# Modulation products: four output tiles side by side in TensorE's column groups, one turn per four tiles

## The chip, the cores and the metric

The kernel runs on one core of a Trainium2 chip. The metric is the device time of one execution in microseconds (us), lower being better; the median of several runs is compared. The engines named below are TensorE (PE, its weight loads shown apart as PEld), VectorE (DVE), ScalarE (ACT), GpSimd (POOL) and the queue of SyncE (SPq) that issues the loads.

## The reference, cut to what matters

The reference is a first block (a mixer and a product-key layer of 128 x 128 experts) for 256 tokens, and after it a second block of two layers whose norms and residuals are modulated by two conditioning vectors. Only the modulation matters here:

```python
silu_c = jax.nn.silu(c)            # [1, 1024]
silu_cc = jax.nn.silu(c_ctx)       # [1024]
for i in range(DEPTH_2):           # two layers
    mod_l = (silu_c @ ada_w[i] + ada_b[i])[:, None, :]       # ada_w[i] is 1024 x 6144
    mod_c = (silu_cc @ ada_w[i] + ada_b[i])[None, None, :]
    sh1_l, sc1_l, g1_l, sh2_l, sc2_l, g2_l = jnp.split(mod_l, N_MOD, axis=-1)
    ...
```

So two rows of 1024 numbers are multiplied by a matrix of 1024 x 12288 float32 (48 MB), and the result has to stand in the kernel as columns: `mod[p, layer, block, s]`, 128 outputs across the partitions, `s` being the conditioning vector.

## The kernel before, in words

All weights come through one ring of four buffers, `raw[:, g % 4, :]`, each piece 128 partitions x 1024 float32 (512 KB), in one fixed order that `add_pieces` writes out (L236 to L284). The queue of SyncE issues a piece as soon as the piece four places before it has been used (L287 to L298). Most pieces are "split": ACT rounds them into `whi` (L310), DVE subtracts into `wlo` (L316), and the high and low parts are multiplied by high and low parts of the activations, three matmuls for each product (L494 to L496, L1690 to L1692).

The expert layer is two long stages of 128 groups each. In the key stage (L1427 to L1661) a group is one piece of `peer_u_t`: 24 matmuls of 128 x 256 into one of three banks, then a gelu by ACT (L1511, L1513) which frees the bank; DVE picks the best keys and experts in between (L1560 to L1634), and from group 62 on PE also routes one-hot products (L1482). In the value stage (L1669 to L1733) a group is one piece of `peer_v_t`, 24 matmuls that add into banks 0 to 3; ACT and DVE make `gh` and `gl` from the gated values (L1713, L1726).

The modulation products are woven into these two stages, since their weights come from the same ring. `ada_w` is cut in 24 output tiles of 512 columns. A tile has eight chunks of 128 inputs, in four pieces; a piece holds two chunks x 512 outputs. `KEY_ADA` and `VALUE_ADA` (L75, L76) say behind which group half a tile is worked: 16 halves in the key stage (tiles 0 to 7, every 3.4 groups from group 3), 32 in the value stage (tiles 8 to 23, every 3.6 groups from group 2).

A half (`half_pe`, L698 to L710) is two raw pieces and four matmuls in plain float32. The stationary operand is one chunk of the conditioning vectors, padded from 2 to 32 columns; the moving operand is 512 weights wide. The four matmuls go to the four column groups, that is to PSUM partitions 0, 32, 64 and 96 of one bank, by chunk: chunk `c` goes to group `c % 4`. So after both halves each column group holds a quarter of the sum. ACT copies the bank to SBUF (`row_act`, L726). Then `turn_pe` (L690 to L696) multiplies each 128 columns of this copy by a 0/1 matrix with two columns, which adds the four quarters and turns rows to columns: four matmuls with 128 x 128 stationary and 2 columns moving. The turn of tile `t - 1` follows the second half of tile `t`; the last turn of each stage stands alone two groups after the last half. `out_act` (L728 to L732) copies the columns to `mod` once in each stage.

What waits on what: PE waits for its two raw pieces (L705), for `ada_rows_out` before it writes a bank that it used two tiles ago and before it turns; ACT waits for PE's `raw_used` before its row copy. In the trace every float32 matmul shows as two records, so a half is 8 records of L709, and a turn 8 records of L695.

Of the kernel before, what the change touches and what calls it, by code (L numbers as in the profile page):

```python
# [60 lines left out]
ROPE_THETA = 10000.0  # L61
TT = T + TC

ADA_TILES = LAYERS * N_MOD * D // 512
ADA = (8, ADA_TILES)
KEY_LOT, VALUE_LOT = range(len(ADA))
COLS = 32

# [3 lines left out]
SPLIT = 3  # L72


KEY_ADA = {3 + n * 34 // 10: [(n // 2, n % 2)] for n in range(2 * ADA[KEY_LOT])}  # L75
VALUE_ADA = {2 + n * 36 // 10: [(ADA[KEY_LOT] + n // 2, n % 2)] for n in range(2 * (ADA[VALUE_LOT] - ADA[KEY_LOT]))}  # L76
BATCH = 4
SLICE = 1650
EXP_AT, TURN_AT = 54, 61
# [14 lines left out]
    NV += _w  # L94


CONSTS = [("ident", P), ("ones", P), ("ones64", P), ("iota", P), ("group", 32), ("rows", NSA_G)]
MIX_CONSTS = [("hg_mask", P), ("dist", TB * T), ("cbias", NSA_HEADS * TB * N_CMP), ("cmask", TB * NSA_G * N_CMP)]
CONST_AT, NCONST = {}, 0
for _n, _w in CONSTS:  # L100
# [8 lines left out]
def const_tables():  # L109

    t = {}
    i = np.arange(P)
    t["ident"] = np.eye(P)
    t["ones"] = np.ones((P, P))
    t["ones64"] = (i[:, None] // 64 == i[None, :] // 64) * 1.0
    t["iota"] = np.broadcast_to(i, (P, P))

    t["group"] = (i[:, None] % 32 == np.arange(32)[None, :]) * 1.0
    t["rows"] = (i[:, None] // 32 == np.arange(NSA_G)[None, :]) * 1.0

    s = np.zeros((P, P))
    for m in range(P):
        k = m + 16 if m % 32 < 16 else m - 16
        s[k, m] = -1.0 if m % 32 < 16 else 1.0
    t["swap"] = s

    t["hg_mask"] = ((i[:, None] <= i[None, :]) & (i[:, None] // HG_CHUNK == i[None, :] // HG_CHUNK)) * 1.0
    pos = np.arange(T)
    dist = (pos[:, None] - pos[None, :]).astype(np.float64)

    t["dist"] = np.where(dist >= 0, -dist, NEG).reshape(TB, P, T).transpose(1, 0, 2).reshape(P, -1)
    end = np.arange(N_CMP) * CMP_STRIDE + CMP_LEN - 1
    cd = (pos[:, None] - end[None, :]).astype(np.float64)
    near = np.where(cd >= 0, -cd, NEG).astype(np.float32).reshape(TB, P, 1, N_CMP)
    slopes = (2.0 ** (-8.0 * (np.arange(NSA_HEADS) + 1) / NSA_HEADS)).astype(np.float32).reshape(2, NSA_G, 1)
    t["cbias"] = (near.transpose(1, 0, 2, 3)[:, None] * slopes[None, :, None]).reshape(P, -1)
    t["cmask"] = np.broadcast_to((cd >= 0).reshape(TB, P, 1, N_CMP) * 1.0, (TB, P, NSA_G, N_CMP)).transpose(1, 0, 2, 3).reshape(P, -1)
    half = DH // 2
    inv = (1.0 / (np.float32(ROPE_THETA) ** (np.arange(0, half, 2, dtype=np.float32) / np.float32(half)))).astype(np.float32)
    row = (pos // GRID_W).astype(np.float32)  # L140
    col = (pos % GRID_W).astype(np.float32)
    ang = np.concatenate([np.tile((row[:, None] * inv).T, (2, 1)), np.tile((col[:, None] * inv).T, (2, 1))])
    t["cos"] = np.tile(np.cos(ang), (2, 1))
    t["sin"] = np.tile(np.sin(ang), (2, 1))
    t["rope"] = np.concatenate([t["cos"], t["sin"], t["swap"]], axis=1)

    def table(names):
        return np.ascontiguousarray(np.concatenate([t[n] for n in names], axis=1).astype(np.float32))
    return table([n for n, _ in CONSTS]), table([n for n, _ in MIX_CONSTS]), table(["rope"])

# [14 lines left out]
def build(nc, dr):  # L165

    ctx = ExitStack()
    with ctx:
        def sem(name):
            return ctx.enter_context(nc.semaphore(name))  # L170
# [73 lines left out]
            return first  # L244


        ada_at = [[] for _ in range(ADA_TILES)]

        def add_half(t, half):
            first = add_pieces("ada_t", False, 4 * t + 2 * half, 4 * t + 2 * half + 2)  # L250
            ada_at[t].extend((first, first + 1))

        top_pe = sem("top_pe_step")
        at_in, at_cmp = [], []
        for w in dr["w_in_t"]:
# [7 lines left out]
        at_keys = add_pieces("peer_keys_t", split=False, end=lambda i: (top_pe, 4 * i + 4))  # L263
        for i in range(2, PK_KEYS):
            at_u.append(add_pieces("peer_u_t", a=i, b=i + 1))
            for h in KEY_ADA.get(i - 2, ()):
                add_half(*h)
        at_v = []
        for i in range(PK_KEYS):
            at_v.append(add_pieces("peer_v_t", a=i, b=i + 1))  # L270
            for h in VALUE_ADA.get(i - 2, ()):
                add_half(*h)
        at_ple = add_pieces("ple_gate_t")
        add_pieces("ple_proj_t")
        at_qkv = [None] * LAYERS
# [25 lines left out]
        def piece_loaded(eng, g):  # L301
            eng.wait_ge(raw_loaded[g % RAW], 16 * (g // RAW + 1))
# [378 lines left out]
        class AdaLot:  # L681
# [3 lines left out]
            def __init__(self, lot, cond, rows, banks):  # L685
                self.a, self.b = ADA[lot - 1] if lot else 0, ADA[lot]
                self.cond, self.rows, self.banks = cond, rows, banks
                self.end = ada_at[self.b - 1][-1] + 1

            def turn_pe(self, pe, t):  # L690

                pe.wait_ge(ada_rows_out, t + 1)
                for j in range(4):
                    n = 4 * (t - self.a) + j
                    mm = pe.matmul(ps[:, self.banks[2], 2 * n:2 * n + 2], self.rows[:, t % 2, j * P:j * P + P], k("group", 0, 2), start=True, stop=True)  # L695
                mm.then_inc(ada_turned, 1)  # L696

            def half_pe(self, pe, t, half):  # L698


                if half == 0 and t >= self.a + 2:
                    pe.wait_ge(ada_rows_out, t - 1)
                for i in (2 * half, 2 * half + 1):
                    g = ada_at[t][i]
                    piece_loaded(pe, g)  # L705
                    for j in range(2):
                        c = 2 * i + j
                        q = COLS * (c % 4)
                        mm = pe.matmul(ps[q:q + COLS, self.banks[t % 2], :], self.cond[:, c, :], raw[:, g % RAW, j * 512:j * 512 + 512],  # L709
                                       start=(c < 4), stop=(c >= 4), tile_position=(0, q))  # L710
                    mm.then_inc(raw_used, 1)

            def pe(self, pe):
                for t in range(self.a, self.b):
                    for half in range(2):
                        self.half_pe(pe, t, half)
                    if t > self.a:
                        self.turn_pe(pe, t - 1)
                self.turn_pe(pe, self.b - 1)

            def row_act(self, act, t):

                act.wait_ge(raw_used, pieces[ada_at[t][3]][3] + 1)
                if t >= self.a + 2:
                    act.wait_ge(ada_turned, t - 1)
                act.activation(self.rows[:, t % 2, :], ps[:, self.banks[t % 2], :], ACT.Copy).then_inc(ada_rows_out, 1)  # L726

            def out_act(self, act):  # L728
                a, b = self.a, self.b
                act.wait_ge(ada_turned, b)  # L730
                act.activation(mod[:, :, :, :].rearrange("p l j s -> p (l j s)")[:, 8 * a:8 * b], ps[:, self.banks[2], 0:8 * (b - a)],
                               ACT.Copy).then_inc(ada_out.h, 1)  # L732

            def act(self, act):
                for t in range(self.a, self.b):
                    self.row_act(act, t)
                self.out_act(act)


        mixer = ctx.enter_context(ExitStack())  # L740
# [686 lines left out]
        with nc.Block() as block:  # L1427
# [5 lines left out]
            def _(pe):  # L1433
# [9 lines left out]
                for i in range(GROUPS):  # L1443
# [12 lines left out]
                    if i == min(KEY_ADA):  # L1456
                        pe.wait_ge(top_act, 8)
                        pe.wait_ge(cond_padded, 2)
                    for t, half in KEY_ADA.get(i, ()):
                        key_lot.half_pe(pe, t, half)  # L1460
                        if half and t > key_lot.a:
                            key_lot.turn_pe(pe, t - 1)
                    if i == max(KEY_ADA) + 2:
                        key_lot.turn_pe(pe, key_lot.b - 1)
# [22 lines left out]
            def _(act):  # L1487
# [11 lines left out]
                        ins = act.activation(ohs[:, r % 2, 1, q, :], ohs[:, r % 2, 1, q, :], ACT.Copy, scale=wT[:, t:t + 1])  # L1499
                    ins.then_inc(hot_weighted, 1)  # L1500
                for i in range(GROUPS):
                    for t, half in KEY_ADA.get(i - 1, ()):
                        if half:
                            key_lot.row_act(act, t)
                    if i == max(KEY_ADA) + 3:
                        key_lot.out_act(act)
                    act.wait_ge(piece_used, nu + i + 1)
# [161 lines left out]
        with ExitStack() as own, nc.Block() as block:  # L1669
# [11 lines left out]
            def _(pe):  # L1681
                for i in range(GROUPS):
# [10 lines left out]
                    mm.then_inc(piece_used, 1)  # L1693
                    if i == min(VALUE_ADA):
                        pe.wait_ge(late_cond, 2)
                    for t, half in VALUE_ADA.get(i, ()):
                        value_lot.half_pe(pe, t, half)
                        if half and t > value_lot.a:
                            value_lot.turn_pe(pe, t - 1)
                    if i == max(VALUE_ADA) + 2:  # L1700
                        value_lot.turn_pe(pe, value_lot.b - 1)
# [1 line left out]
            @block.scalar  # L1703
            def _(act):
                for i in range(GROUPS):
                    for t, half in VALUE_ADA.get(i - 3, ()):
                        if half:
                            value_lot.row_act(act, t)
                    if i == max(VALUE_ADA) + 5:
                        value_lot.out_act(act)  # L1710
                    if i >= 3:
# [526 lines left out]
def _layouts(a):  # L2238
# [30 lines left out]
    o["peer_v_t"] = np.ascontiguousarray(f["peer_v"][0].reshape(PK_KEYS, PK_KEYS, D).transpose(1, 0, 2))  # L2269
    o["ple_gate_t"] = _tiles(f["ple_gate_w"][0])  # L2270
    o["ple_proj_t"] = _tiles(f["ple_proj"][0])
    o["ada_t"] = np.concatenate([_tiles(f["ada_w_2"][i]) for i in range(LAYERS)])
    o["qkv0_t"] = _tiles(f["na_w_qkv_2"][0])
    o["o0_t"] = _tiles(f["na_w_o_2"][0])
    g = f["gqa_w_qkv_2"][0]
# [50 lines left out]
```

## Time and profile before

| | |
|---|---|
| median of 3 runs | 2252.4 us (2251.59 to 2254.49) |
| the profiled execution, own time | 2255.02 us |
| its span | 2253.2 us |
| its mean granted TensorE clock | 0.973 |
| PE busy | 2130.6 us (95%) |
| DVE busy | 1252.7 us (56%) |
| ACT busy | 1033.1 us (46%) |
| load traffic | 325.76 MB read, 145 GB/s over the span |

Busy times are of one profiled execution. A matmul record is longer than the time by which it holds up the next one, since matmuls are pipelined (most records of 128 x 256 last 0.28 us and follow each other every 0.12 us), so the cost of a matmul is read from starts, not from durations. PE's "busy 95%" says where it has no gap, and the stages have to be looked at one by one.

### The profile page before, as it was taken

To read this page: it belongs to the slowest core of one execution; us is meant where nothing else is said; L and a number is where in the kernel's file an instruction comes from. 1 tells how busy PE (TensorE), PEld (TensorE's weight loads), DVE (VectorE), ACT (ScalarE), POOL (GpSimd) and SP (SyncE) were. 2 spreads that over 40 slices of the span, in tenths; PEclk is the share of its full clock that TensorE was granted. 3 is DMA by queue.
4 is the path that set the end of the run, shared out by engine and by line. 5 is a ranking of instruction groups with operands and counts; after the bars stand their busy time and mean duration, and the time that the engine had idled before them with its cause. 6 is when DMAs were issued, how large, how long until landed. Compare 5 with 4: busy or idle time off the path is not lost. (4 is left out here: it accounts for less than half of the span.)

```text
span 2253.2 us, 36524 instructions
## 1 busy us (share of the span) xinstructions
PE 2130.6 (95%) x15218; PEld 1892.8 (84%) x15218; DVE 1252.7 (56%) x1943; ACT 1033.1 (46%) x1914; POOL 7.0 (0%) x10
## 2 busy tenths in 40 slices
PE   7888999999999999999988999989999998899998
PEld 6768999999998999999986876768887887479997
DVE  6675588877887445445455237553333225556544
ACT  5664444467775444444444227442322215455443
POOL 0000000000000000000000000000000000100000
PEclk9988999999999999999989999999999999899999
DMA  6503577744443777777644210123222223014543
GB/s 206 189 1 129 175 256 246 252 168 141 141 141 122 247 246 246 249 250 238 233 162 154 95 66 1 57 75 103 92 97 92 94 85 118 1 58 150 187 172 109
DMA packets 91252, 329.18 MB, mean 146 GB/s; under 512 B 10064, under 2 KB 12496, under 8 KB 90832
## 3 DMA queue, kind: packets, MB, share of 16 engines
q1 hardware_dynamic: 91088, 326.84, 42.6%
q8 instruction: 121, 1.98, 0.4%
q14 instruction: 43, 0.35, 0.1%
HBM read 325.76 MB, written 1.05 MB: 145 GB/s over the span
## 5 line engine op out<-in xcount | busy, mean ns | idle before, releaser
L316 DVE TENSOR_TENSOR wlo<-raw,whi 128x1024 fp32r<-128x1024 f32 (+1 forms) x502 | 612.2, 1221 | 604.0 <-ACT whi L310 599.9
L310 ACT ACTIVATE whi<-raw 128x1024 fp32r<-128x1024 f32 (+1 forms) x502 | 527.1, 1052 | 485.0 <-PE ps L496 460.4
L494 PE MATMUL ps<-x_hi,whi 128*128 128x512 f32 (+1 forms) x1040 | 360.4, 347 | 28.1 <-DVE x_lo L477 22.6
L495 PE MATMUL ps<-x_lo,whi 128*128 128x512 f32 (+1 forms) x1040 | 359.3, 345 | 0.0
L496 PE MATMUL ps<-x_hi,wlo 128*128 128x512 f32 (+1 forms) x1040 | 358.8, 345 | 0.0
L494 PE MATMUL ps<-xT_hi,whi 128*128 128x256 f32 x1152 | 334.0, 290 | 4.1 <-DVE xT_lo L475 4.1
L495 PE MATMUL ps<-xT_lo,whi 128*128 128x256 f32 x1152 | 326.7, 284 | 0.0
L496 PE MATMUL ps<-xT_hi,wlo 128*128 128x256 f32 x1152 | 326.7, 284 | 0.0
L1690 PE MATMUL ps<-gh,whi 128*128 128x256 f32 x1024 | 294.1, 287 | 5.6 <-DVE gl L1726 5.6
L1691 PE MATMUL ps<-gl,whi 128*128 128x256 f32 x1024 | 290.8, 284 | 0.0
L1692 PE MATMUL ps<-gh,wlo 128*128 128x256 f32 x1024 | 290.7, 284 | 0.0
L494 PEld LDWEIGHTS ps<-x_hi,whi 128*128 128x128 f32 x1040 | 202.1, 194 | 53.8 <-issue 31.5
L494 PEld LDWEIGHTS ps<-xT_hi,whi 128*128 128x128 f32 x1152 | 221.7, 192 | 12.1 <-issue 11.2
L495 PEld LDWEIGHTS ps<-xT_lo,whi 128*128 128x128 f32 x1152 | 221.9, 193 | 0.0
L496 PEld LDWEIGHTS ps<-xT_hi,wlo 128*128 128x128 f32 x1152 | 221.6, 192 | 0.0
L496 PEld LDWEIGHTS ps<-x_hi,wlo 128*128 128x128 f32 x1040 | 202.0, 194 | 22.7
L495 PEld LDWEIGHTS ps<-x_lo,whi 128*128 128x128 f32 x1040 | 202.1, 194 | 21.9
L1690 PEld LDWEIGHTS ps<-gh,whi 128*128 128x128 f32 x1024 | 197.6, 193 | 20.0 <-issue 20.0
L1691 PEld LDWEIGHTS ps<-gl,whi 128*128 128x128 f32 x1024 | 197.7, 193 | 0.0
L1692 PEld LDWEIGHTS ps<-gh,wlo 128*128 128x128 f32 x1024 | 197.6, 193 | 0.0
L1713 ACT ACTIVATE gh<-gated 128x256 fp32r<-128x256 f32 x128 | 53.0, 416 | 192.6 <-PE ps L1692 190.4
L1726 DVE TENSOR_TENSOR gl<-gated,gh 128x256 fp32r<-128x256 f32 x128 | 54.4, 426 | 140.5 <-ACT gh L1713 140.5
(346 smaller groups left out, 3088.1 us busy)
## 6 DMA issues: line engine op xcount, KB each, us to landing
raw<-peer_u_t SPq DMA_DIRECT2D x128, 512.0 KB, 3.3
raw<-peer_v_t SPq DMA_DIRECT2D x128, 512.0 KB, 4.3
raw<-ada_t SPq DMA_DIRECT2D x96, 512.0 KB, 5.3
raw<-ffn_in_t SPq DMA_DIRECT2D x88, 512.0 KB, 3.2
raw<-ffn_out_t SPq DMA_DIRECT2D x44, 512.0 KB, 3.2
raw<-qkv_t SPq DMA_DIRECT2D x36, 512.0 KB, 3.3
raw<-w_in_t SPq DMA_DIRECT2D x24, 512.0 KB, 3.7
raw<-peer_wq_t SPq DMA_DIRECT2D x16, 512.0 KB, 3.3
```

The costliest lines, as they stand in the source:

```text
L310: act.activation(whi[:, n % SPLIT, 0:w], raw[:, g % RAW, 0:w], ACT.Copy).then_inc(hi_done, 1)
L316: dve.tensor_tensor(wlo[:, n % SPLIT, 0:w], raw[:, g % RAW, 0:w], whi[:, n % SPLIT, 0:w].bitcast(F32), ALU.subtract).then_inc(lo_done, 1)
L494: pe.matmul(place, wh, xh, start=start, stop=False, skip_group_check=shared)
L495: pe.matmul(place, wh, xl, start=False, stop=False, skip_group_check=shared)
L496: return pe.matmul(place, wl, xh, start=False, stop=stop, skip_group_check=shared)
L1690: pe.matmul(place, w[0], gh[:, i % 3, :], start=(i == 0 and c % 2 == 0), stop=False, skip_group_check=True)
L1691: pe.matmul(place, w[0], gl[:, i % 3, :], start=False, stop=False, skip_group_check=True)
L1692: mm = pe.matmul(place, w[1], gh[:, i % 3, :], start=False, stop=(i == GROUPS - 1), skip_group_check=True)
L1713: act.activation(gh[:, i % 3, :], gbuf[:, i, :], ACT.Copy).then_inc(gates_hi, 1)
L1726: dve.tensor_tensor(gl[:, i % 3, :], gbuf[:, i, :], gh[:, i % 3, :].bitcast(F32), ALU.subtract).then_inc(gates_lo, 1)
```

## The change

The same products are laid out another way. Four output tiles (2048 outputs, a "quad") are worked together, six quads in all, two in the key stage and four in the value stage. A piece now holds one chunk of 128 inputs x 1024 outputs, that is two tiles' worth. A unit is two such pieces and four matmuls with the same stationary chunk, one for each tile of the quad, each in its own column group. Over the eight units of a quad every column group adds up its own whole sum. The row copy and the turn come once in a quad; the turn's 0/1 matrix has eight columns ("spots", which picks rows 32q and 32q + 1), so it gives 128 outputs x 4 tiles x 2 vectors in one matmul. The places of the units (`KEY_ADA`, `VALUE_ADA`), the number and size of the pieces, and their order in the ring are those of the halves. The copy to `mod` is one ACT instruction per quad, with a strided view. The table of constants grows by 8 columns. On the host the weights are laid out for it.

```diff
-ADA_TILES = LAYERS * N_MOD * D // 512
-ADA = (8, ADA_TILES)
+QUAD = 4 * 512
+QUADS = LAYERS * N_MOD * D // QUAD
+ADA = (2, QUADS)
...
-KEY_ADA = {3 + n * 34 // 10: [(n // 2, n % 2)] for n in range(2 * ADA[KEY_LOT])}
-VALUE_ADA = {2 + n * 36 // 10: [(ADA[KEY_LOT] + n // 2, n % 2)] for n in range(2 * (ADA[VALUE_LOT] - ADA[KEY_LOT]))}
+KEY_ADA = {3 + n * 34 // 10: divmod(n, C) for n in range(C * ADA[KEY_LOT])}
+VALUE_ADA = {2 + n * 36 // 10: divmod(C * ADA[KEY_LOT] + n, C) for n in range(C * (ADA[VALUE_LOT] - ADA[KEY_LOT]))}
...
+    t["spots"] = (i[:, None] == 32 * (n // 2) + n % 2) * 1.0
...
+            def unit_pe(self, pe, t, c):
+                if c == 0 and t >= self.a + 2:
+                    pe.wait_ge(ada_rows_out, t - 1)
+                for i in range(2):
+                    g = ada_at[t, c] + i
+                    piece_loaded(pe, g)
+                    for j in range(2):
+                        q = COLS * (2 * i + j)
+                        mm = pe.matmul(ps[q:q + COLS, self.banks[t % 2], :], self.cond[:, c, :], raw[:, g % RAW, j * 512:j * 512 + 512],
+                                       start=(c == 0), stop=(c == C - 1), tile_position=(0, q))
+                    mm.then_inc(raw_used, 1)
...
             def turn_pe(self, pe, t):
                 pe.wait_ge(ada_rows_out, t + 1)
                 for j in range(4):
-                    n = 4 * (t - self.a) + j
-                    mm = pe.matmul(ps[:, self.banks[2], 2 * n:2 * n + 2], self.rows[:, t % 2, j * P:j * P + P], k("group", 0, 2), start=True, stop=True)
+                    at = 32 * (t - self.a) + 8 * j
+                    mm = pe.matmul(ps[:, self.banks[2], at:at + 8], self.rows[:, t % 2, j * P:j * P + P], k("spots"), start=True, stop=True)
                 mm.then_inc(ada_turned, 1)
...
-                act.activation(mod[:, :, :, :].rearrange("p l j s -> p (l j s)")[:, 8 * a:8 * b], ps[:, self.banks[2], 0:8 * (b - a)],
-                               ACT.Copy).then_inc(ada_out.h, 1)
+                for t in range(a, b):
+                    to = mod[:, :, :, :].rearrange("p l j s -> p (l j s)")[:, 32 * t:32 * t + 32].rearrange("p (q j s) -> p q j s", q=4, j=4)
+                    got = ps[:, self.banks[2], 32 * (t - a):32 * (t - a) + 32].rearrange("p (j q s) -> p q j s", j=4, q=4)
+                    ins = act.activation(to, got, ACT.Copy)
+                ins.then_inc(ada_out.h, 1)
...
-                    for t, half in KEY_ADA.get(i, ()):
-                        key_lot.half_pe(pe, t, half)
-                        if half and t > key_lot.a:
+                    if i in KEY_ADA:
+                        t, c = KEY_ADA[i]
+                        key_lot.unit_pe(pe, t, c)
+                        if c == 1 and t > key_lot.a:
                             key_lot.turn_pe(pe, t - 1)
...
-                    for t, half in KEY_ADA.get(i - 1, ()):
-                        if half:
-                            key_lot.row_act(act, t)
+                    if i - 1 in KEY_ADA and KEY_ADA[i - 1][1] == C - 1:
+                        key_lot.row_act(act, KEY_ADA[i - 1][0])
```

The value stage is changed in the same way, its row copy standing three groups behind the unit as before. `row_act` waits for the last piece of chunk 7.

## Rows read from the trace of the kernel before

**Rows 1.** The page's slices: 40 equal parts of the span, busy tenths, granted clock.

```profile
PE   7888999999999999999988999989999998899998
PEclk9988999999999999999989999999999999899999
```

**Rows 2.** Stages: busy us (x instructions) of each engine, clock, DMA share, GB/s.

```profile
260.00:457.00 197.00, 197.00 (x1623) 181.46 (x1623) 163.05 (x464) 90.80 (x135) 0.00 (x0) 1.00 0.73 247
457.00:724.00 267.00, 261.55 (x2220) 261.34 (x2218) 211.58 (x272) 184.57 (x532) 0.00 (x0) 1.00 0.41 141
735.00:1113.00 378.00, 378.00 (x3102) 346.91 (x3102) 187.05 (x227) 162.62 (x242) 0.00 (x0) 1.00 0.73 247
1149.00:2253.00 1104.00, 1028.89 (x6154) 858.89 (x6154) 499.88 (x678) 435.75 (x727) 6.84 (x6) 0.96 0.28 97
```

**Rows 3.** All instructions of the turn's line: ns min/median/max, first and last start.

```profile
L695 PE MATMUL ps<-kon,values_rows x128: 169/251/272, 768.9 to 1112.8; 128*128 128x2 f32 x128
L695 PE MATMUL ps<-kon,gated x64: 169/251/272, 311.2 to 456.3; 128*128 128x2 f32 x64
```

**Rows 4.** PE in order of time (start us, us): a half without a turn.

```profile
745.13 0.28 PE L1692 MATMUL ps<-gh,wlo 128*128 128x256 f32 x1
745.34 1.07 PE L709 MATMUL ps<-raw,values_cond 128*32 128x512 f32 x8
746.34 0.38 PE L1690 MATMUL ps<-gh,whi 128*128 128x256 f32 x1
746.56 0.28 PE L1691 MATMUL ps<-gl,whi 128*128 128x256 f32 x1
746.68 0.28 PE L1692 MATMUL ps<-gh,wlo 128*128 128x256 f32 x1
```

**Rows 5.** PE in order of time: a half with a turn behind it.

```profile
767.65 0.28 PE L1692 MATMUL ps<-gh,wlo 128*128 128x256 f32 x1
767.86 1.07 PE L709 MATMUL ps<-raw,values_cond 128*32 128x512 f32 x8
768.86 1.05 PE L695 MATMUL ps<-kon,values_rows 128*128 128x2 f32 x8
769.77 0.36 PE L1690 MATMUL ps<-gh,whi 128*128 128x256 f32 x1
769.98 0.28 PE L1691 MATMUL ps<-gl,whi 128*128 128x256 f32 x1
770.09 0.28 PE L1692 MATMUL ps<-gh,wlo 128*128 128x256 f32 x1
```

**Rows 6.** PE in order of time: a turn that stands alone.

```profile
455.48 0.28 PE L496 MATMUL ps<-xT_hi,wlo 128*128 128x256 f32 x1
455.60 0.95 PE L695 MATMUL ps<-kon,gated 128*128 128x2 f32 x8
456.41 0.36 PE L494 MATMUL ps<-xT_hi,whi 128*128 128x256 f32 x1
...
456.73 0.28 PE L496 MATMUL ps<-xT_hi,wlo 128*128 128x256 f32 x1
```

**Rows 7.** PE in order of time: four float32 matmuls with 128 columns moving.

```profile
478.09 0.28 PE L496 MATMUL ps<-xT_hi,wlo 128*128 128x256 f32 x1
478.21 1.06 PE L1482 MATMUL ps<-one_hots 128*128 128x128 f32 x8
479.02 0.36 PE L494 MATMUL ps<-xT_hi,whi 128*128 128x256 f32 x1
```

**Rows 8.** PE, 50.8 to 52.6 us: float32 matmuls of 512 columns, full width.

```profile
50.91 1.88 PE L820 MATMUL ps<-head_rstd,kon 128*128 128x512 f32 x4
```

**Rows 9.** ACT's row copy and final copy, each line's instructions.

```profile
L726 ACT ACTIVATE values_rows<-ps x16: 597/597/602, 746.5 to 1105.5; 128x512 f32<-128x512 f32 x16
L731 ACT ACTIVATE mod<-ps x2: 216/246/277, 457.0 to 1113.1; 128x64 f32<-128x64 f32 x1, 128x128 f32<-128x128 f32 x1
```

**Rows 10.** Waits, value stage then key stage: us in total, times, longest us.

```profile
ACT gh L1713 <- PE ps L1692: 170.5, 97, 2.7
ACT whi L310 <- DMA raw<-peer_v_t: 2.6, 4, 1.8
...
ACT whi L310 <- DMA raw<-peer_u_t: 7.0, 11, 0.8
```

**Rows 11.** DVE and PE in order of time around value group 12.

```profile
761.44 1.23 DVE L316 TENSOR_TENSOR wlo<-raw,whi 128x1024 fp32r<-128x1024 f32 x1 [2.41 <-ACT whi L310]
764.89 0.28 PE L1690 MATMUL ps<-gh,whi 128*128 128x256 f32 x1
```

**Rows 12.** Two modulation pieces: their issue (with time to landing), and their use.

```profile
999.40 1.62 SPq L298 DMA_DIRECT2D raw<-ada_t  x2
raw<-ada_t SPq DMA_DIRECT2D x2, 512.0 KB, 7.1
1007.55 0.28 PE L1692 MATMUL ps<-gh,wlo 128*128 128x256 f32 x1
1007.76 1.11 PE L709 MATMUL ps<-raw,values_cond 128*32 128x512 f32 x8
```

**Rows 13.** DVE at the end of its selection work, which PE needs at 468.00 us.

```profile
462.80 0.43 DVE L1633 TENSOR_TENSOR gated<-gated 128x256 f32<-128x256 f32 x1
463.80 1.23 DVE L316 TENSOR_TENSOR wlo<-raw,whi 128x1024 fp32r<-128x1024 f32 x1 [0.58 <-ACT whi L310]
```

More of the change, by code:

```diff
@@ L94 @@
     NV += _w
-CONSTS = [("ident", P), ("ones", P), ("ones64", P), ("iota", P), ("group", 32), ("rows", NSA_G)]
+CONSTS = [("ident", P), ("ones", P), ("ones64", P), ("iota", P), ("group", 32), ("rows", NSA_G), ("spots", 8)]
 MIX_CONSTS = [("hg_mask", P), ("dist", TB * T), ("cbias", NSA_HEADS * TB * N_CMP), ("cmask", TB * NSA_G * N_CMP)]
@@ L118, in const_tables @@
     t["group"] = (i[:, None] % 32 == np.arange(32)[None, :]) * 1.0
+    n = np.arange(8)
+    t["spots"] = (i[:, None] == 32 * (n // 2) + n % 2) * 1.0
     t["rows"] = (i[:, None] // 32 == np.arange(NSA_G)[None, :]) * 1.0
@@ L244, in add_pieces, with add_unit @@
             return first
[L247 to L251, printed above, removed]
+        ada_at = {}
+        def add_unit(u):
+            t, c = u
+            ada_at[u] = add_pieces("ada_t", False, 2 * (C * t + c), 2 * (C * t + c) + 2)
         top_pe = sem("top_pe_step")
@@ L265, in build @@
             at_u.append(add_pieces("peer_u_t", a=i, b=i + 1))
-            for h in KEY_ADA.get(i - 2, ()):
-                add_half(*h)
+            if i - 2 in KEY_ADA:
+                add_unit(KEY_ADA[i - 2])
         at_v = []
@@ L270, in build @@
             at_v.append(add_pieces("peer_v_t", a=i, b=i + 1))
-            for h in VALUE_ADA.get(i - 2, ()):
-                add_half(*h)
+            if i - 2 in VALUE_ADA:
+                add_unit(VALUE_ADA[i - 2])
         at_ple = add_pieces("ple_gate_t")
@@ L687, in __init__ @@
                 self.cond, self.rows, self.banks = cond, rows, banks
-                self.end = ada_at[self.b - 1][-1] + 1
+            def unit_pe(self, pe, t, c):
[9 more added lines that the diff above has]
+                    mm.then_inc(raw_used, 1)
             def turn_pe(self, pe, t):
@@ L693, in turn_pe @@
                 for j in range(4):
-                    n = 4 * (t - self.a) + j
-                    mm = pe.matmul(ps[:, self.banks[2], 2 * n:2 * n + 2], self.rows[:, t % 2, j * P:j * P + P], k("group", 0, 2), start=True, stop=True)
+                    at = 32 * (t - self.a) + 8 * j
+                    mm = pe.matmul(ps[:, self.banks[2], at:at + 8], self.rows[:, t % 2, j * P:j * P + P], k("spots"), start=True, stop=True)
                 mm.then_inc(ada_turned, 1)
[L698 to L719, printed above, removed]
             def row_act(self, act, t):
-                act.wait_ge(raw_used, pieces[ada_at[t][3]][3] + 1)
+                act.wait_ge(raw_used, pieces[ada_at[t, C - 1] + 1][3] + 1)
                 if t >= self.a + 2:
@@ L730, in out_act @@
                 act.wait_ge(ada_turned, b)
-                act.activation(mod[:, :, :, :].rearrange("p l j s -> p (l j s)")[:, 8 * a:8 * b], ps[:, self.banks[2], 0:8 * (b - a)],
-                               ACT.Copy).then_inc(ada_out.h, 1)
[L734 to L737, printed above, removed]
+                for t in range(a, b):
[3 more added lines that the diff above has]
+                ins.then_inc(ada_out.h, 1)
         mixer = ctx.enter_context(ExitStack())
@@ L1695, in _ @@
                         pe.wait_ge(late_cond, 2)
-                    for t, half in VALUE_ADA.get(i, ()):
-                        value_lot.half_pe(pe, t, half)
-                        if half and t > value_lot.a:
+                    if i in VALUE_ADA:
+                        t, c = VALUE_ADA[i]
+                        value_lot.unit_pe(pe, t, c)
+                        if c == 1 and t > value_lot.a:
                             value_lot.turn_pe(pe, t - 1)
@@ L1705, in _ @@
                 for i in range(GROUPS):
-                    for t, half in VALUE_ADA.get(i - 3, ()):
-                        if half:
-                            value_lot.row_act(act, t)
+                    if i - 3 in VALUE_ADA and VALUE_ADA[i - 3][1] == C - 1:
+                        value_lot.row_act(act, VALUE_ADA[i - 3][0])
                     if i == max(VALUE_ADA) + 5:
@@ L2271, in _layouts @@
     o["ple_proj_t"] = _tiles(f["ple_proj"][0])
-    o["ada_t"] = np.concatenate([_tiles(f["ada_w_2"][i]) for i in range(LAYERS)])
+    ada = np.concatenate([f["ada_w_2"][i] for i in range(LAYERS)], axis=1)
+    o["ada_t"] = np.ascontiguousarray(ada.reshape(C, P, QUADS, 2, 2 * 512).transpose(2, 0, 3, 1, 4).reshape(-1, P, PIECE))
     o["qkv0_t"] = _tiles(f["na_w_qkv_2"][0])
```

## The prediction, made before the changed kernel ran

> **What bounds the kernel now.** I went from the page's slices to the stages, then to single instructions. The slices show TensorE (PE) nearly full everywhere, and full where the modulation products run [rows 1]. By stage, PE is busy for 197.00 of 197.00 us in the key stage's part with halves and for 378.00 of 378.00 us in the value stage's, at the full granted clock (1.00, the 2.4 GHz level), while DVE has 163.05 and 187.05 us, ACT 90.80 and 162.62 us, and the loads take 0.73 of the DMA engines' time [rows 2]. The reader should see that no other engine is near its limit there and that PE has no gap at all. The order of time confirms it: matmuls of 128 x 256 start every 0.12 us, and what stands between two groups is a half, a turn, or nothing [rows 4 to 6]. So in these two stretches the time is the sum of PE's instructions, and anything taken from PE is gained, as long as nothing else is late by then.
>
> **What the change removes: 18 turns.** The trace has 128 records of the turn's line in the value stage and 64 in the key stage [rows 3]; a turn is 8 records, so there are 16 and 8 turns, 24 in all. After the change there is one for each quad: 4 and 2. Twelve turns go from the value stage and six from the key stage. All 18 are of the kind that stands behind a half; the two at the ends, which stand alone, stay.
>
> **The price of a turn** comes from starts, since durations overlap. A half without a turn: from the last matmul of the group before it (745.13) to the third of the group after it (746.68) are 1.55 us, where three steps of 0.12 would be 0.36, so a half costs 1.19 us [rows 4]. With a turn the same stretch goes from 767.65 to 770.09, 2.44 us, so half and turn cost 2.08 us [rows 5]. The difference, the turn, is 0.89 us. The turn that stands alone gives the same: 455.48 to 456.73 is 1.25 us, less 0.36 is 0.89 us [rows 6]. The agreement matters: the turn costs what it costs whether it follows a half or not, so nothing of it stays behind with the half. The rows shown are typical of all 26 halves without and 22 with a turn. 18 x 0.89 = 16.0 us.
>
> The Trainium skill's page "TensorE: Matmul & The Clock Gate", section "LDWEIGHTS (loading the stationary operand)", puts a weight load at its columns divided by 1.2, in ns. By that, a turn's eight loads of 128 columns would be 8 x 107 = 0.85 us, and the gain, called an estimate, 15.4 us. The trace's 0.89 us decides.
>
> **What it adds to the turns that stay: eight moving columns for two.** The trace has no such matmul. Bounds: a float32 matmul with 2 columns on the one side, one with 128 on the other. Four of the latter (one-hot products) take the stretch from 478.09 to 479.02, 0.93 us [rows 7]; the lone turn has the same 0.93 us from 455.48 to 456.41 [rows 6]. Both ends are equal, so eight columns cost nothing more. Six turns stay; the term is zero.
>
> **What it changes in the 48 halves, now units.** Number, size, places and column groups of the matmuls stay: four in a row to partitions 0, 32, 64, 96 of one bank. New are that all four load the same stationary chunk, and that seven of eight units add to the bank where it was one of two halves. In the value stage every matmul from the second group on adds to its bank, and it keeps the 0.12 us of the key stage's, whose groups begin afresh [rows 4, 6]. So adding is free at that shape. For loading one chunk four times the trace has no row; the nearest is a half itself, four chunks in four groups, 1.19 us. A gain is excluded, since the same 512 columns have to stream; the upper bound is the loss of the overlap among column groups. Full-width float32 matmuls of 512 columns follow each other with four records in 1.88 us, of which the last runs out in 0.59: (1.88 - 0.59) / 3 = 0.43 us each [rows 8]. Eight records in a row would be 3.4 us, 2.2 us more for each unit. I take zero, since the row that is nearest is the same instruction at the same places.
>
> **What it takes from ACT.** 18 of 24 row copies of 0.60 us, some 10.7 us, and it makes six final copies of 32 columns where there were two, of 64 and 128 columns in 0.22 and 0.28 us [rows 9]; so at most 6 x 0.28 = 1.7 us. None of it shows. ACT sat idle 170.5 us for PE in the value stage [rows 10], and the copies' cover is that wait. The four final copies of the value stage, at most 1.1 us where 0.28 was, stand ahead of `gh` and a `whi` in ACT's queue, and DVE and PE wait for those; they meet a PE that is ahead of nothing, because the split weights are ready 2.2 us or more before their group. Without that cover they would cost about 0.8 us once.
>
> **The waits.** No wait is new. PE still waits for a row copy before a turn, two units after the last product of that tile, some seven groups, and ACT needs 0.60 us for it. PE's wait on a bank used two tiles ago becomes one on a bank used two quads ago, which is longer past. Nothing is moved past SPq or POOL; the ring has the same 96 pieces in the same order.
>
> **What is late next.** With 16 us less on PE, the followers have less time. First the split weights: at value group 12 `wlo` is done at 761.44 + 1.23 = 762.67 and PE comes at 764.89, a margin of 2.2 us, the smallest of that stage; the usual one is 3 to 5 us [rows 11]. ACT had waited 1.8 us for a transfer there, the longest of four such waits [rows 10]. Second, the modulation pieces themselves, which have no buffer ahead. At the tightest place the second was issued at 999.40 + 1.62 - 0.33 = 1000.7, took 7.1 us and so landed at 1007.8, just as PE came for it: 1007.76 where a half normally follows 0.21 us after the last matmul, and the records took 1.11 for 1.07 us [rows 12, 4]. That place, and every second half, has no turn since the half before it, and so shows what all will be like after the change. PE lost 0.05 us there and nothing at the other 23. So removing turns makes the other half of the places like those that already hold without loss. Mean traffic goes from 247 GB/s to 247 x 575 / 559 = 254 GB/s [rows 2]. Third, DVE's selection work, which PE needs for its transposes at 468.00: it is done at 462.80 + 0.43 = 463.23, 4.8 us earlier, and DVE follows PE there, waiting for `whi` after it [rows 13]. PE will be 6 x 0.89 = 5.3 us earlier at that point, but DVE's pace is set by PE's through each `whi`, and it waited for ACT again and again on the way; its 163.05 us of work fit into 197.0 - 5.3 = 191.7 us [rows 2].
>
> **The sum.** The profiled execution took 2255.02 us and would take 2239.0. It is 2.6 us above the median of 2252.4, so the median would be 2252.4 - 16.0 = 2236.4 us.
>
> **What shakes it.** After the value stage the clock is 0.96 over 1104 us [rows 2], that is 88 us at the 1.2 GHz level in several stretches, each behind a wait of PE. All of this comes 16 us earlier, and a stretch may end sooner or later. The three runs differ by 2.9 us without any change. I allow 2.5 us to either side. The Trainium skill ("TensorE: Matmul & The Clock Gate", "What you observe") says likewise that the moment of the rise differs from run to run; no row here tells its share.
>
> **Rivals.**
> (a) *The transfers take part of it back.* For it: one piece landed as PE came [rows 12], and landings vary. Against: 23 of 24 like places had time to spare. If a quarter of the 48 units waited 0.5 us, 6 us would be lost: 2242 us. Chance 0.10.
> (b) *The loads set the pace after all*, and the two stretches cannot shrink: 2252 us. Against: 0.73 of the DMA engines' time, and ACT's waits for transfers are only 2.6 and 7.0 us, with no gap on PE behind them [rows 2, 10]. This is also the case that the change does nothing. Chance 0.02.
> (c) *Slower: the four column groups no longer overlap in a unit*, because all four load the same chunk. Price 2.2 us for each of 48 units, 106 us: 2342 us; it decides from (16.0 + 4.5) / 48 = 0.43 us for each unit. Against: column groups, bank and order are those of before, where the overlap is seen: eight records of 0.6 us in 1.07 us [rows 4]. Chance 0.03.
> (d) *More than forecast*: the half-clock stretches get shorter, and PE's margins elsewhere with them: 2231 us. Chance 0.05.
> The forecast itself: 0.80, with a range of 2234 to 2239.
>
> **How the numbers follow.** The likeliest is 2236.4. Taking in the run-to-run spread, a part of (a) and a part of (d), the range is 2232 to 2241. A measurement of this kernel can tell about 0.2% from no change, 4.5 us. Faster: 0.80 + 0.10 + 0.05 = 0.95, of which I give 0.01 to same for a stronger form of (a); same 0.03, slower 0.03 make the rest.
>
> **What the profile after would show.** L695's successor has 48 records in place of 192, with unchanged 0.93 us stretches; halves still cost 1.19 us; both stretches stay at 100% PE, the value part about 10.7 us and the key part 5.3 us shorter; traffic near 254 GB/s; everything behind the value stage unchanged but for the clock. Gaps on PE ahead of the unit's matmuls would speak for (a), a longer unit for (c). The prediction is wrong if either appears in more than a few units.

## The result, and the profile after

The changed kernel takes 2222.8 us (median of 4 runs, 2219.66 to 2224.46) against 2253.4 us before (4 runs on the same occasion, 2251.59 to 2255.33). The ratio is 0.9861, with a 95% interval of 0.9845 to 0.9876. It is 30.7 us faster, nearly twice the 16.0 us that were forecast, and below the forecast range, whose lower end was 2232.

| | before | after |
|---|---|---|
| profiled execution, own time, us | 2255.02 | 2222.13 |
| its span, us | 2253.2 | 2220.4 |
| PE busy, us | 2130.6 | 2098.9 |
| ACT busy, us | 1033.1 | 1030.9 |
| instructions | 36524 | 36186 |
| mean granted clock | 0.973 | 0.974 |

The page after, its slices as in [rows 1], and three stretches as in [rows 2]:

```profile
PE   7888999999998999999979999989999998899998
PEclk9998999999999999999989999999999999899999
```

```profile
260.00:457.00 197.00, 197.00 (x1644) 180.54 (x1643) 170.07 (x466) 91.75 (x135) 0.00 (x0) 1.00 0.75 251
735.00:1113.00 378.00, 374.22 (x3126) 344.05 (x3126) 199.48 (x244) 169.99 (x248) 0.00 (x0) 1.00 0.76 252
1149.00:2253.00 1104.00, 1003.20 (x5927) 817.99 (x5925) 477.02 (x640) 417.85 (x693) 6.85 (x6) 0.97 0.28 92
```

The stretches have the bounds of before, so that they now hold more of the work. What to see is the first: PE is full for 197.00 us as it was, but holds 1644 matmul records instead of 1623, although turns are gone. (A turn is 8 records in 0.89 us, denser than a group, so fewer turns alone would lower the count.) The second is not full because the value stage is over at 1107.9 us. The third ends beyond the kernel's end.

The turn, as in [rows 3], and one that stands alone, as in [rows 6]:

```profile
L711 PE MATMUL ps<-kon,values_rows x32: 173/256/277, 816.6 to 1074.2; 128*128 128x8 f32 x32
L711 PE MATMUL ps<-kon,gated x16: 172/256/277, 368.6 to 442.4; 128*128 128x8 f32 x16
```

```profile
441.55 0.28 PE L499 MATMUL ps<-xT_hi,wlo 128*128 128x256 f32 x1
441.67 0.95 PE L711 MATMUL ps<-kon,gated 128*128 128x8 f32 x8
442.48 0.36 PE L497 MATMUL ps<-xT_hi,whi 128*128 128x256 f32 x1
```

There are 48 records for 192, six turns for 24, and from 441.55 to 442.48 the stretch still takes 0.93 us with eight columns. A unit, as in [rows 4]:

```profile
771.42 0.28 PE L1683 MATMUL ps<-gh,wlo 128*128 128x256 f32 x1
771.63 1.06 PE L702 MATMUL ps<-raw,values_cond 128*32 128x512 f32 x8
772.62 0.39 PE L1681 MATMUL ps<-gh,whi 128*128 128x256 f32 x1
772.85 0.28 PE L1682 MATMUL ps<-gl,whi 128*128 128x256 f32 x1
772.97 0.28 PE L1683 MATMUL ps<-gh,wlo 128*128 128x256 f32 x1
```

From 771.42 to 772.97 are 1.55 us, as with a half before. So the parts that the prediction costed are as it said. What is new is in the groups themselves, which the change does not touch. First and last matmul of key group 26, before and then after:

```profile
351.23 0.28 PE L494 MATMUL ps<-xT_hi,whi 128*128 128x256 f32 x1
...
353.99 0.28 PE L496 MATMUL ps<-xT_hi,wlo 128*128 128x256 f32 x1
```

```profile
342.75 0.28 PE L497 MATMUL ps<-xT_hi,whi 128*128 128x256 f32 x1
...
345.44 0.28 PE L499 MATMUL ps<-xT_hi,wlo 128*128 128x256 f32 x1
```

The 23 steps from the first to the 24th matmul take 2.76 us before and 2.69 after, 0.120 and 0.117 us each. The duration of one matmul, 0.28 us, does not show it; only the starts do. Taken over all some 2900 undisturbed steps of each stage, the mean goes from 119.8 to 116.8 ns in the key stage and from 119.9 to 116.8 in the value stage.

Where the 32.8 us of the two profiled spans are, by the starts of first and last matmuls: before the projection of the keys 4.7 us, in that projection 1.1, in the key stage 13.3 (452.05 to 438.74), in the value stage 20.4 (423.26 to 402.85); and the second block takes 6.6 us more (1095.77 to 1102.35). So part of the gain lies ahead of the modulation products, where nothing was changed, and the second block, where nothing was changed either, lost.

The clock has a share in it that the mean granted clock, 0.973 and 0.974, hardly shows. The profile's clock records put 123.7 us of the span before at the 1.2 GHz level and 115.8 us of the span after. These 7.9 us less are worth at most half as much, 4.0 us, where PE was busy, since that level is half the other; 2.5 of them fall into the value stage and 3.7 into the second block. Of the 4.7 us ahead of the projection, the shorter step explains some 1.6: 615 undisturbed steps of 256 columns there take 119.8 ns before and 117.2 after. The rest is not shown to be the change's, since that part of the kernel varies from run to run: where its buffers lie as before, it took 209.4 us here, and 210.4, 207.0, 208.9 and 207.7 in the profiled executions of `no_shift`, `shift256`, `shift512` and `moving32` below.

### The profile page after: what moved, and what is told of

Read it like the earlier page. It is cut to its first block and busy times, and to the rows that moved or that the text cites. A ratio compares the mean times of both kernels' runs of the same rounds, so it can differ in the third digit from the quotient of the medians.

```text
span 2220.4 us, 36186 instructions
## 1 busy us (share of the span) xinstructions
PE 2098.9 (95%) x15074; PEld 1844.0 (83%) x15074; DVE 1250.9 (56%) x1943; ACT 1030.9 (46%) x1900; POOL 7.1 (0%) x10
## 5 line engine op out<-in xcount | busy, mean ns | idle before, releaser
L497 PE MATMUL ps<-ffn_hi,whi 128*128 128x512 f32 (+1 forms) x352 | 119.8, 340 | 6.2 <-PEq L541 6.2
```

Source lines behind the costliest of these rows:

```text
L497: pe.matmul(place, wh, xh, start=start, stop=False, skip_group_check=shared)
```

## The experiments

The change does one thing besides what its text is about: the table of constants, `kon`, gets 8 columns, so every buffer placed behind it starts 32 bytes later. The ring `raw` and the split weights `whi` and `wlo` lie ahead of it and stay. Theory A was that these 32 bytes make the matmuls quicker; theory B that the new products or the missing turns do.

**The shift without the change.**

```diff
-CONSTS = [..., ("group", 32), ("rows", NSA_G)]
+CONSTS = [..., ("group", 32), ("rows", NSA_G), ("unused", 8)]
```

> The kernel before with 8 unused columns in the table of constants: all buffers allocated behind it start 32 bytes later, as in the changed kernel; the halves and the 24 turns are those of before. Theory A (the 32 bytes make the 128x256 matmuls follow each other faster): their step falls from 0.120 to 0.117 us in the key and value stages, some 6100 matmuls x 0.003 = 18 us there, and the time is about 2253.4 - 14.4 = 2239 us, with the turns still at 0.89 us each. Theory B (the faster step comes from the new products or from having fewer turns): step 0.120 us and 2253 us.

Measured: 2238.4 us (4 runs), ratio 0.9940 (0.9917 to 0.9962). The key stage took 442.95 us, the value stage 414.47, the mean steps were 116.8 and 116.9 ns. Value group 97, first and last matmul:

```profile
1027.85 0.28 PE L1691 MATMUL ps<-gh,whi 128*128 128x256 f32 x1
...
1030.53 0.28 PE L1693 MATMUL ps<-gh,wlo 128*128 128x256 f32 x1
```

It takes 2.68 us for 23 steps, with all 24 turns in place. That is what theory A expected.

**The change without the shift.** The eight columns of the 0/1 matrix are columns of the identity, which is in the table already.

```diff
-CONSTS = [..., ("rows", NSA_G), ("spots", 8)]
+CONSTS = [..., ("rows", NSA_G)]
...
-  mm = pe.matmul(ps[:, self.banks[2], at:at + 8], self.rows[...], k("spots"), start=True, stop=True)
+  mm = pe.matmul(ps[:, self.banks[2], at:at + 8].rearrange("p (q s) -> p q s", s=2), self.rows[...],
+                 k("ident").rearrange("p (q r) -> p q r", r=COLS)[:, :, 0:2], start=True, stop=True)
```

> The changed kernel, its 0/1 matrix taken as a strided view of the identity that is in the table anyway (columns 32q and 32q + 1), so that no column is added and every buffer starts where it does in the kernel before. Theory A: the step of the 128x256 matmuls is back at 0.120 us, only the 18 turns are gone, 2253.4 - 16.0 = 2237.4 us. Theory B: 0.117 us and 2223 us, as the changed kernel.

Measured: 2237.1 us (4 runs) beside 2254.7 before, ratio 0.9926 (0.9906 to 0.9947). The same group:

```profile
1037.09 0.28 PE L1680 MATMUL ps<-gh,whi 128*128 128x256 f32 x1
...
1039.85 0.28 PE L1682 MATMUL ps<-gh,wlo 128*128 128x256 f32 x1
```

2.76 us for 23 steps, mean 119.8 and 119.9 ns. So the change proper gives what the prediction said it would, and the shift gives the rest. The two ratios multiply to 0.9940 x 0.9926 = 0.9866, the changed kernel's 0.9861.

**Which distance counts.** Four larger shifts, one kernel that moves weights and activations alike, and one that moves the weights alone:

> The kernel before with 16 unused columns in the table, a shift of 64 bytes. If what matters is the start within 64 bytes, the step is back at 0.120 us and the time at 2253 us. If any other start than that of before is faster, the step is 0.117 us and the time about 2239 us.

> The kernel before with 32 unused columns, a shift of 128 bytes for everything behind the table. If the distance counts modulo 256, as the looks at 256 and 512 bytes suggest, the key stage takes 446 us or less and the step is below 0.118 us; if it counts modulo 128, 0.120 us and 452 us.

> The kernel before with 64 unused columns, a shift of 256 bytes for everything behind the table. The distance between weights and activations was a multiple of 512 bytes. If only a multiple of 512 is slow, the step is 0.117 or 0.118 us and the key stage about 445 us; if multiples of 256 are, 0.120 us and 452 us.

> The kernel before with 128 unused columns, a shift of 512 bytes. The chunks of the weights are 512 bytes apart and those of the activations 1024, and the step was 0.120 us for all of them; so if the distance modulo 512 matters, the step is 0.120 us again and the key stage 452 us. If every shift helps, 0.117 us and 443 to 446 us.

```diff
# all32
+        ctx.enter_context(nc.sbuf_tensor("unused", [P, 8], F32))
         raw = ctx.enter_context(nc.sbuf_tensor("raw", [P, RAW, PIECE], F32))
```

> The kernel before with 32 unused bytes ahead of the ring of weights: the weights (stationary) and the activations (moving) both start 32 bytes later, so their distance is that of before. If the distance between the two operands matters, the step stays at 0.120 us and the time at 2253 us. If the moving operand's own start matters, the step is 0.117 us and the time about 2239 us.

```diff
# weights32
+        idle = ctx.enter_context(nc.sbuf_tensor("idle", [P, 1], F32))
         whi = ctx.enter_context(nc.sbuf_tensor("whi", [P, SPLIT, PIECE], F32R))
...
-        idle = ctx.enter_context(nc.sbuf_tensor("idle", [P, 1], F32))
```

> The kernel before, with one small buffer (idle) moved from behind the table to ahead of the split weights whi and wlo: the weights, the stationary operand, start 32 bytes later, and the activations start where they did. If the distance between the two operands matters, the step of the 128x256 matmuls falls to about 0.117 us and the key stage from 452 to about 443 us. If the moving operand's own start matters, 0.120 us and 452 us.

The table gives the mean step in the key stage (256 columns moving, some 2900 steps), the mean step of the matmuls with 512 columns moving over split weights in the second block (some 2160 steps), and the stages' times in us, all from the starts in each trace. The last column is one run where no median is named:

| activations against weights | 256 cols, ns | 512 cols, ns | key stage | second block | us |
|---|---|---|---|---|---|
| as before | 119.8 | 226.8 | 452.05 | 1095.8 | 2253.4 (median) |
| both +32 bytes (all32) | 119.8 | 226.8 | 452.04 | 1094.1 | 2249.9 |
| +32 (shift32) | 116.8 | 233.3 | 442.95 | 1099.9 | 2238.4 (median) |
| +64 (shift64) | 117.6 | 228.9 | 445.60 | 1089.8 | 2234.4 |
| +128 (shift128) | 119.3 | 232.6 | 450.28 | 1105.1 | 2256.7 |
| +256 (shift256) | 119.8 | 226.7 | 452.04 | 1095.8 | 2252.6 |
| +512 (shift512) | 119.8 | 226.8 | 452.04 | 1095.9 | 2255.0 |
| -32 (weights32) | 118.3 | 233.3 | 447.16 | 1105.1 | 2249.3 |

The steps can be compared as they stand. The times of the second block can't, since its time at the 1.2 GHz level differs too: 75.2 us before, but 64.3 with the shift of 32 bytes, 65.4 with 64 and 69.2 in `all32`, against 70.9 to 75.2 in the other four. So some 5 of the 6.0 us that the second block gains at 64 bytes go with the clock, and the 2234.4 us, one run, are not a price of the distance alone. Why the clock fell less often there is open.

Value group 97 with a shift of 256 bytes, and with everything moved by 32:

```profile
1046.36 0.28 PE L1691 MATMUL ps<-gh,whi 128*128 128x256 f32 x1
...
1049.12 0.28 PE L1693 MATMUL ps<-gh,wlo 128*128 128x256 f32 x1
```

```profile
1045.29 0.28 PE L1691 MATMUL ps<-gh,whi 128*128 128x256 f32 x1
...
1048.05 0.28 PE L1693 MATMUL ps<-gh,wlo 128*128 128x256 f32 x1
```

It is 2.76 us both times. The step does not hang on the activations' own address, since 32 bytes for all change nothing, and 32 bytes for the weights alone do. It hangs on the distance between weights and activations, and it has the old values again at 256 and 512 bytes, so the distance counts modulo 256 as far as these shifts tell; modulo 128 is excluded by the 232.6 ns at 128 bytes. Before, it was an exact multiple: by the buffers' addresses in the program `xT_hi` started 159744 bytes behind `whi`, 624 x 256, and `gh` lay at the same place as `xT_hi`. At 128 bytes I expected a step below 0.118 us if 256 was the period, and that was a miss: 119.3 ns.

What is good for 256 columns is bad for 512. Two matmuls of the second block 24 steps apart, before and then with the shift of 32 bytes:

```profile
1503.83 0.39 PE L494 MATMUL ps<-x_hi,whi 128*128 128x512 f32 x1
...
1509.27 0.39 PE L494 MATMUL ps<-x_hi,whi 128*128 128x512 f32 x1
```

```profile
1483.08 0.39 PE L495 MATMUL ps<-x_hi,whi 128*128 128x512 f32 x1
...
1488.68 0.39 PE L495 MATMUL ps<-x_hi,whi 128*128 128x512 f32 x1
```

These are 5.44 and 5.60 us, 226.7 and 233.3 ns a step. The second block has some 2350 undisturbed steps of 512 columns and 2200 of 256, so the shift costs it 2350 x 6.5 = 15.3 us and gives 2200 x 3.1 = 6.8. The difference is 8.5 us. The changed kernel's second block took 6.6 us more, beside 3.7 us less at the 1.2 GHz level, which hid up to 1.8 us of it: 8.4 us together.

**The moving operand alone.** To tell the operands of the matmul from the other buffers behind the table, above all the gated values that ACT and DVE write meanwhile:

```diff
+        pb("unused1", [P, 8])
         ffn_norm.parts = xH = [pb(n, [P, C, T], F32R) for n in ("xT_hi", "xT_lo")]
...
+            own.enter_context(nc.sbuf_tensor("unused2", [P, 8], F32))
             gh = own.enter_context(nc.sbuf_tensor("gh", [P, 3, T], F32R))
```

> The kernel before with 32 unused bytes ahead of the two moving operands alone, xT_hi and xT_lo in the key stage, gh and gl in the value stage. Every other buffer of the two stages starts where it did, the gated values and the second block's among them. If it is the distance between moving operand and weights, the step is 0.117 us in both stages, the key stage takes 443 us and the value stage 414 us, and the whole 2253 - 9.1 - 8.8 - 1.0 for the projection ahead of them = 2234 us, the second block staying at 1096 us. If it is the place of another buffer (the gated values, which ACT and DVE write), 0.120 us and 2253 us.

Measured: 2232.8 us (4 runs), ratio 0.9909 (0.9892 to 0.9925). Key stage 443.26 us, value stage 415.57, steps 116.8 and 117.0 ns; the second block's steps are 120.0 and 226.8 ns, unchanged. The gated values, the ring and the split weights had not moved. By the program's addresses some small buffers had, other than the expectation says: those placed behind the two operands (`keyT`, `wT` and `one_hots` in the key stage, `values_rows` and `values_cond` in the value stage). The last two are read only in halves and turns, while the step is shorter in the groups between them. `moving32`, `weights32` and `all32` together leave the distance between the moving operand and the weights.

**Only the low parts.**

```diff
-        ffn_norm.parts = xH = [pb(n, [P, C, T], F32R) for n in ("xT_hi", "xT_lo")]
+        ffn_norm.parts = xH = [pb("xT_hi", [P, C, T], F32R)]
+        pb("unused1", [P, 8])
+        xH.append(pb("xT_lo", [P, C, T], F32R))
...
+            own.enter_context(nc.sbuf_tensor("unused2", [P, 8], F32))
             gl = own.enter_context(nc.sbuf_tensor("gl", [P, 3, T], F32R))
```

> The kernel before with only the low parts, xT_lo and gl, 32 bytes later; the high parts stay. Of the three matmuls of a product (whi with the high part, whi with the low part, wlo with the high part) only the second streams a shifted operand. If a matmul that streams holds up the load of the next one's weights by their distance, the step behind or onto this one matmul is shorter than 0.120 us and the others stay; a third of the gain, some 3 us for each stage (449 and 420 us). If the pace is set by something common to all, all three steps change or none.

Measured: 2235.2 us, key stage 446.24, value stage 415.49. The three steps of a product in the key stage, in order: 117.9, 119.6 and 116.2 ns, where all were 119.6 to 120.1 before. In the value stage they are 117.1, 118.3 and 116.1 ns, for 119.8 to 120.0 before. So moving the operand of one matmul in three changed two of the steps in one stage and all three in the other, and the gain is two thirds in the key stage and nearly all in the value stage. Neither expectation fits; which read holds up which stays open.

**Can both be had?** Two kernels. The first is the changed one at 64 bytes, where 256 columns gain and 512 lose little:

```diff
-CONSTS = [..., ("rows", NSA_G), ("spots", 8)]
+CONSTS = [..., ("rows", NSA_G), ("spots", 8), ("unused", 8)]
```

> The changed kernel with 8 unused columns more in the table, so that the buffers behind it start 64 bytes later than in the kernel before and 32 later than in the changed one. If the two effects add up: the single look at a shift of 64 bytes gave 2234.4 us with the old products, less 16.0 us for 18 turns is 2218 us, some 4 us below the changed kernel's 2222.8. If the turns and the shift share a gain (a rival: the faster step leaves other work late, so that part of a turn's time is lost), nearer to 2223 us or above.

Measured: 2219.0 us (4 runs), ratio 0.9855 (0.9831 to 0.9878). The second has no column added, and 32 bytes at the head of the two scopes that end before the second block:

```diff
         mixer = ctx.enter_context(ExitStack())
+        mixer.enter_context(nc.sbuf_tensor("unused1", [P, 8], F32))
...
         peer = ctx.enter_context(ExitStack())
+        peer.enter_context(nc.sbuf_tensor("unused2", [P, 8], F32))
```

> The changed products with the view of the identity (no column added), and 32 unused bytes at the head of the first block's buffers and of the expert layer's, which are given back before the second block's are placed. So the first block and the expert layer have their activations 32 bytes off the weights' multiple of 256, and the second block has them on it. If the shift is a gain for 256 columns moving and a loss for 512, as the looks at 32 bytes show (0.120 to 0.117 us, but 0.226 to 0.233 us), the second block keeps its 1096 us and the rest is that of the changed kernel: 2222.8 - 6.6 = 2216 us. If the 6.6 us had another cause (the clock's stretches), 2223 us.

Measured: 2219.1 us (5 runs, 2213.41 to 2220.70), ratio 0.9844 (0.9827 to 0.9860). Its steps are 116.7 and 116.8 ns in the key and value stages and 226.7 ns for 512 columns, and the second block takes 1095.5 us. So the 6.6 us came back where they were expected. The whole is 3 us above the expectation, of which 2.4 are in the part ahead of the projection (207.1 us against 204.7 in the changed kernel). The traces say where: the same matmul starts at 114.5 and 114.2 us, and a later one at 141.3 and 138.6, and from 114 to 142 us the mean granted clock is 0.82 here and 0.93 there. So these 2.4 us go with the clock and not with the placing. The intervals of these two and of the changed kernel overlap; none of the three is shown to be the fastest.

## Why the prediction was wrong, point by point

**The bound.** Right. PE's records leave no gap in the two stages, but for late pieces that only the starts show (below), and what was taken from it was gained.

**18 turns at 0.89 us.** Right. 48 records are left. The kernel with the turns gone and nothing shifted took 2237.1 us where 2236.4 was forecast, and on its own occasion 17.6 us less than before, with an interval of 12 to 21 from the ratio. The lone turn costs what it did [rows 6].

**Eight moving columns for nothing.** Right: the stretch of the lone turn is 0.93 us, as with 2 and with 128 columns [rows 6, 7].

**The unit at a half's price.** Right: 1.55 us from 771.42 to 772.97, as in [rows 4]. Rival (c), the loss of the overlap, did not come.

**ACT.** Right as far as it shows: its row copies fell from 24 to 6, and no wait for a row copy appeared on PE.

**What is late next.** Rival (a) came in a small size. In the changed kernel PE stood before or within three units for their second piece, 1.92 us in all; without the shift, in six units, 2.84 us; with all 24 turns in place and the shift of 32 bytes in one, 0.16 us, and in the kernel before in one, 0.05 us. The trace names the transfer:

```profile
L702 PE MATMUL ps<-raw,gated x128: 592/605/617, 271.8 to 435.4; 128*32 128x512 f32 x128
its engine sat idle before it (us, times) until:
  DMA raw<-ada_t: 1.5, 3
```

The longest of them, PE in order of time; the second piece was issued at 307.27 and took 6.7 us:

```profile
312.89 0.28 PE L499 MATMUL ps<-xT_hi,wlo 128*128 128x256 f32 x1
313.10 1.95 PE L702 MATMUL ps<-raw,gated 128*32 128x512 f32 x8
```

It is 1.95 us for 1.07. The argument that the places without a turn ahead of them already show what all will be like [rows 12] was too kind: two intervals without a turn in a row leave less time to catch up than one did. That is a reading, and the late pieces alone don't show it: kernels with all 24 turns lost between nothing and 1.42 us (`moving32`, three units) in one trace each, those with six turns between 1.11 (`after64`) and 2.84 us. ACT's waits for transfers in 735 to 1113 us say it more clearly, where [rows 10] had 2.6 us in four:

```profile
ACT whi L313 <- DMA raw<-peer_v_t: 29.1, 30, 2.8
```

With the turns gone and no shift it is 18.8 us in 26, with the shift and all turns 5.9 us in seven. The size of what PE lost was within the 6 us that the rival allowed.

**The step that failed** is one that the prediction doesn't have. The section on the change says that the table of constants grows by 8 columns; the prediction gave this no term, not even a zero with a bound. Its sum, 2252.4 - 16.0, and its line that everything behind the value stage would be unchanged but for the clock both rest on that silence. It took the 0.12 us of the other matmuls as given, because the change does not touch them. It does: it moves their operands. Some 6100 steps in the two stages at 3.0 to 3.1 ns each are 9.2 + 9.5 = 18.7 us, more than the 16 us of the turns, and the second block gave part of it back. The account of the key stage is now: 6 turns x 0.89 = 5.3 us, 3072 steps x 3.0 ns = 9.2 us, less 1.2 us of late pieces, 13.3 us, and 13.3 were measured. In the value stage: 12 x 0.89 = 10.7, 3072 x 3.1 ns = 9.5, about 1.2 from 2.5 us less at the 1.2 GHz level (PE is busy there, so the lower level costs half its time), less 0.75 of a late piece, 20.6 us, and 20.4 were measured. Ahead of these stages the same steps are faster (1.6 and 1.1 us, see the result), and in the second block the 512-column ones slower.

The Trainium skill's page "SBUF — State Buffer", section "Who interferes with whom", gives PE two independent read ports, one for the moving operand and one for the weight load. Read so, the place of one against the other would change nothing. The runs here disagree, 116.8 against 119.8 ns, and they decide; they don't show that it is the ports where the two meet.

**The range** allowed 2.5 us for the clock and some for late pieces and had nothing for a cause that I had not listed. Rival (d), "more than forecast", named the clock. It had a small part: 7.9 us less at the 1.2 GHz level in the profiled execution, at most 4.0 us. Without the shift the changed kernel took 2237.1 us, inside the range, so the miss is the step's.

## What to carry to other kernels

A buffer that grows by a few bytes moves every buffer behind it, and this belongs in the list of a change's parts with a price of its own; here it was worth about as much as what the change was made for (ratios 0.9940 and 0.9926). When a stream of matmuls sets the time, read its step from starts, over thousands of them, and compare it between the two kernels before looking for anything else. And before the credit goes to the idea of a change, run its side effect alone and the change without it.

## What the runs showed of the hardware

The step of back-to-back matmuls, each with its own weight load, hangs on the distance in SBUF between the moving operand and the weights. At a multiple of 256 bytes 256 float32r columns take 119.8 ns and 512 take 226.8 ns. At 32 bytes more it is 116.8 and 233.3, at 64 bytes 117.6 and 228.9, at 128 bytes 119.3 and 232.6, at 32 bytes less 118.3 and 233.3. No other distance was run. Moving both alike changes nothing. So there is no one best distance among these: it is another one for 256 columns than for 512. That two reads of the array meet in some part of the memory is my reading; the run with only the low parts moved, which changed two steps of three in one stage and all three in the other, did not tell which reads these are.

A float32 matmul with a 128 x 128 weight load took the same time with 2, 8 and 128 columns moving, 0.11 us for each of its two records (0.93 us for the stretch of four such matmuls in each case).
